# Odd attention of a hybrid encoder: maps combined unnormalised, the RMS norm of each head moved to VectorE, and the first four heads projected ahead of the last four

## What is computed

```python
def one_block(qblk):
    scores = jnp.einsum('bhqd,bhkd->bhqk', qblk, k).astype(F32) * (hd ** -0.5)
    p = jax.nn.softmax(scores, axis=-1).reshape(bsz, h, 2, C_Q_BLOCK, s)
    a = (p[:, :, 0] - lam * p[:, :, 1]).astype(v.dtype)
    return jnp.einsum('bhqk,bhkd->bhqd', a, v)
...
return rms_norm(out, subln_w) * (1.0 - lambda_init)     # per head, over 128 channels
...
return merge_heads(o) @ w_out                            # output projection, 1024 x 1024
```

## Time and profile before

| what | value |
|---|---|
| median of 3 runs | 1373.25 us (1370.11 to 1374.86) |
| the profiled execution, its own time | 1379.12 us |
| its span, first to last instruction | 1377.2 us |
| mean granted TensorE clock | 0.964 |
| odd attention, first combine to last | 502.36 to 533.06 us |
| output projection, first product to last | 546.20 to 570.68 us |

### The profile page before, as it was taken

The page is one execution under the profiler, slowest core; times in us unless marked ns, Lnnn a source line. Parts: engine busy times, 40 slices in busy tenths (PEclk is TensorE's granted clock), DMA queues, the critical chain, the costliest instruction groups (busy, mean ns, idle before and its releaser), DMA issues.

```text
span 1377.2 us, 20147 instructions
## 1 busy us (share of the span) xinstructions
PE 1298.9 (94%) x7164; PEld 1183.8 (86%) x7164; DVE 1069.3 (78%) x1006; ACT 835.8 (61%) x870; POOL 127.1 (9%) x112
## 2 busy tenths in 40 slices
PE   5997899999899986899999999999999999999996
PEld 4887888999787865789899899899998998998984
DVE  4777756544546996778889889889889898898997
ACT  3555342434433463357777777777777777787773
POOL 1035011000001832110000000000000000000000
PEclk9998959999999997889999999999999999999998
DMA  9653027766436540689999999999999999999990
GB/s 337 186 186 94 1 76 259 247 180 192 154 108 191 166 146 1 229 285 385 342 391 377 352 398 358 367 398 346 378 395 337 396 387 346 392 353 359 399 358 32
DMA packets 231280, 374.75 MB, mean 272 GB/s; under 512 B 8784, under 2 KB 156368, under 8 KB 231104
## 3 DMA queue, kind: packets, MB, share of 16 engines
q1 hardware_dynamic: 225344, 351.50, 72.8%
q0 software_dynamic: 5888, 22.61, 4.4%
HBM read 363.07 MB, written 11.01 MB: 272 GB/s over the span
## 4 chain that ended last, share of the span: by engine, by line
PE 85%; DVE 10%; issue 2%; ACT 2%; DMA 1%; POOL 0%; SPq 0%; DVEq 0%; ACTq 0%
PE psum L323 24%; PE psum L325 24%; PE psum L324 24%; DVE wlo L304 4%; PE psum L1710 1%; DMA raw<-in_ev_w_in 1%; PE psum L1528 1%; PE psum L1356 1%; PE psum L1355 1%; PE psum L1354 1%; PE psum L1464 1%; PE psum L1444 1%; PE psum L1512 1%; PE psum L1339 1%; PE psum L1377 1%
## 5 line engine op out<-in xcount | busy, mean ns | idle before, releaser
L304 DVE TENSOR_TENSOR wlo<-raw,whi 128x1408 fp32r<-128x1408 f32 (+2 forms) x493 | 785.4, 1612 | 209.3 <-ACT whi L297 205.6
L297 ACT CAST whi<-raw 128x1408 fp32r<-128x1408 f32 (+2 forms) x493 | 653.2, 1331 | 300.0 <-PE psum L325 275.7
L323 PE MATMUL psum<-whi,xe_hi 128*128 128x352 f32 x1024 | 332.6, 325 | 1.6 <-DVE mv L1299 1.6
L325 PE MATMUL psum<-whi,xe_lo 128*128 128x352 f32 x1024 | 330.7, 323 | 0.0
L324 PE MATMUL psum<-wlo,xe_hi 128*128 128x352 f32 x1024 | 330.5, 323 | 0.0
L323 PEld LDWEIGHTS psum<-whi,xe_hi 128*128 128x128 f32 x1024 | 192.4, 188 | 2.1 <-issue 1.8
L324 PEld LDWEIGHTS psum<-wlo,xe_hi 128*128 128x128 f32 x1024 | 192.4, 188 | 0.3
L325 PEld LDWEIGHTS psum<-whi,xe_lo 128*128 128x128 f32 x1024 | 192.5, 188 | 0.0
L323 PE MATMUL psum<-whi,xT_hi 128*128 128x512 f32 (+1 forms) x464 | 168.2, 363 | 8.4 <-DVE wlo L304 7.0
L324 PE MATMUL psum<-wlo,xT_hi 128*128 128x512 f32 (+1 forms) x464 | 167.5, 361 | 0.0
L325 PE MATMUL psum<-whi,xT_lo 128*128 128x512 f32 (+1 forms) x464 | 167.1, 360 | 0.0
(11 more groups left out here) (281 smaller groups left out, 1289.0 us busy)
## 6 DMA issues: line engine op xcount, KB each, us to landing
raw<-in_od_w SPq DMA_DIRECT2D x256, 704.0 KB, 6.9
raw<-in_od_w SPq DMA_DIRECT2D x94, 768.0 KB, 6.3
raw<-in_ev_w SPq DMA_DIRECT2D x32, 704.0 KB, 4.2
raw<-in_ev_w_in SPq DMA_DIRECT2D x32, 512.0 KB, 5.0
raw<-in_od_w SPq DMA_DIRECT2D x30, 512.0 KB, 6.1
raw<-in_od_w_in SPq DMA_DIRECT2D x24, 512.0 KB, 4.2
raw<-in_ev_w SPq DMA_DIRECT2D x12, 768.0 KB, 4.4
raw<-in_ev_w_out SPq DMA_DIRECT2D x8, 512.0 KB, 4.6
```

The lines of the kernel that those rows point to most:

```text
L297: nc.scalar.copy(into[j][:, 0:kc * n], src[:, 0:kc * n]).then_inc(hi_done, 1)
L304: nc.vector.tensor_tensor(into[j][:, 0:kc * n], src[:, 0:kc * n], high[j][:, 0:kc * n].bitcast(F32), ALU.subtract).then_inc(lo_done, 1)
L323: nc.tensor.matmul(ps, hi[:, k, t0:t0 + P], w_h, start=(k == first_k), stop=False)
L325: last = nc.tensor.matmul(ps, lo[:, k, t0:t0 + P], w_h, start=False, stop=(k == last_k))
```

## The change

The maps are combined unnormalised: with d0 and d1 the sums of a row's two maps, the new map is e1 * (-lambda * d0 / d1) + e0, which is the old one times d0. The factor is taken back in the norm: the sum of squares is multiplied by 1 / d0 squared before the power, and the result of the power by 1 / d0 after it. So `combine` has one small product and one full combination for each row tile and no scaling. The power stays on GpSimd, for both groups of four heads with 8 values per row (`hms`, `hrs`); the multiplication by it and by the gain is now one VectorE instruction for each head and row tile (`normal_heads`), for both groups. The heads are turned and split in two lots (`turn_heads`, `mixed_hi`, `mixed_lo`): the first four after the last values, then tile 0 of the projection (which needs only the first two heads), then the last four heads, then tiles 1 to 3. ScalarE squares the last four heads behind the copies of the first four, and casts tile 0 of the second weight group ahead of the copies of the last four.

```diff
@@ GpSimd @@
-            rms_heads(1, on2, sub[:, None, None, :].broadcast_to([P, NT, 4, 128]), proj2[:, :, 0:512])
-            for t in range(NT):
-                pool.wait_ge(r_ms, 3 + t)
-                rsqrt(vec[:, 40 + 4 * t:44 + 4 * t], vec[:, 32 + 4 * t:36 + 4 * t], 1.0 / AD).then_inc(r_rs, 1)
+            for g in range(2):
+                pool.wait_ge(h_ms, g + 1)
+                rsqrt(hrs[:, g].rearrange("p t h -> p (t h)"), hms[:, g].rearrange("p t h -> p (t h)"), 1.0 / AD).then_inc(h_pw, 1)
@@ ScalarE: map_exps, and behind the head loop @@
-                                         accum_out=vec[:, 48 + 4 * p + u:49 + 4 * p + u]).then_inc(c_e, 1)
+                                         accum_out=den[:, h, u:u + 1]).then_inc(c_e, 1)
...
+            def mixed_hi(g):
+                for t in range(NT):
+                    act.wait_ge(t_ps, 16 + 2 * g + t + 1)
+                    nc.scalar.copy(by_bank(xT_hi, 2 * t + g), psum[:, 4 + 2 * g + t, :].rearrange("p (k s) -> p k s", s=P)).then_inc(t_hi, 1)
+
+            mixed_hi(0)
             act.wait_ge(c_av, 8)
-            act.wait_ge(heads_out, 2)
+            act.wait_ge(h_ms, 1)
             for t in range(NT):
                 nc.scalar.activation(sq2[:, t], psum[:, 6 + t, :].rearrange("p (h c) -> p h c", h=4), ACT.Square).then_inc(r_sq, 1)
-            transposed_hi(4)
-            split_hi(act, Q_OUT2, 1, G_SQ)
+            split_hi(act, Q_OUT2, 1, G_SQ, js=(0,))
+            mixed_hi(1)
+            split_hi(act, Q_OUT2, 1, G_SQ, js=(1, 2, 3))
@@ VectorE: combine @@
-                link(nc.vector.reciprocal(vec[:, 64 + 4 * p:68 + 4 * p], vec[:, 48 + 4 * p:52 + 4 * p]))
-                link(nc.vector.tensor_scalar(vec[:, 80 + 2 * p:82 + 2 * p], vec[:, 66 + 4 * p:68 + 4 * p], vec[:, 92:93], None, ALU.mult))
-                for t in range(NT):
-                    link(nc.vector.tensor_scalar(eP[p][:, 1, t, :], eP[p][:, 1, t, :], vec[:, 80 + 2 * p + t:81 + 2 * p + t], None, ALU.mult))
-                    ins = nc.vector.scalar_tensor_tensor(aP[p][:, t, :], eP[p][:, 0, t, :], vec[:, 64 + 4 * p + t:65 + 4 * p + t],
-                                                         eP[p][:, 1, t, :], ALU.mult, ALU.add)
+                link(nc.vector.reciprocal(rden[:, h, :], den[:, h, :]))
+                link(nc.vector.scalar_tensor_tensor(cmap[:, h, :], rden[:, h, 2:4], vec[:, 92:93], den[:, h, 0:2], ALU.mult, ALU.mult))
+                for t in range(NT):
+                    ins = nc.vector.scalar_tensor_tensor(aP[p][:, t, :], eP[p][:, 1, t, :], cmap[:, h, t:t + 1],
+                                                         eP[p][:, 0, t, :], ALU.mult, ALU.add)
@@ VectorE: the norm @@
+            def mean_squares(g):
+                dve.wait_ge(r_sq, 2 + 2 * g)
+                r0 = rden[:, 4 * g:4 * g + 4, 0:2].rearrange("p h t -> p t h")
+                nc.vector.tensor_tensor(hrs[:, g], r0, r0, ALU.mult)
+                link(nc.vector.tensor_reduce(hms[:, g], sq2, AX_X, ALU.add))
+                nc.vector.tensor_tensor(hms[:, g], hms[:, g], hrs[:, g], ALU.mult).then_inc(h_ms, 1)
+
+            def normal_heads(g):
+                dve.wait_ge(h_pw, g + 1)
+                r0 = rden[:, 4 * g:4 * g + 4, 0:2].rearrange("p h t -> p t h")
+                link(nc.vector.tensor_tensor(hrs[:, g], hrs[:, g], r0, ALU.mult))
+                for t in range(NT):
+                    for h in range(4):
+                        col = g * 512 + h * 128
+                        values = psum[:, 6 + t, h * 128:h * 128 + 128] if g else on2[:, t, h, :]
+                        ins = nc.vector.scalar_tensor_tensor(proj2[:, t, col:col + 128], values, hrs[:, g, t, h:h + 1], sub[:],
+                                                             ALU.mult, ALU.mult)
+                    ins.then_inc(mix_done, 1)
...
                 if h == 5:
-                    sum_squares(1, sq2)
-            dve.wait_ge(heads_out, 2)
-            for t in range(NT):
-                dve.wait_ge(r_sq, 3 + t)
-                nc.vector.tensor_reduce(vec[:, 32 + 4 * t:36 + 4 * t], sq2[:, t], AX_X, ALU.add).then_inc(r_ms, 1)
...
-            transposed_lo(4)
+                    mean_squares(0)
+            normal_heads(0)
+            mixed_lo(0)
+            mean_squares(1)
+            normal_heads(1)
+            mixed_lo(1)
             split_lo(dve, Q_OUT2, 1, G_SQ)
@@ TensorE @@
-            pe.wait_ge(heads_out, 2)
-            transpose_chunks(lambda k, t: proj2[:, t, k * P:(k + 1) * P], mixed=2)
-            square_block(Q_OUT2, 0, 0, turned=20)
+            def turn_heads(g):
+                for t in range(NT):
+                    pe.wait_ge(mix_done, 2 + 2 * g + t + 1)
+                    for kk in range(4):
+                        k = 4 * g + kk
+                        ins = nc.tensor.transpose(psum[:, 4 + 2 * g + t, kk * P:(kk + 1) * P], proj2[:, t, k * P:(k + 1) * P], ident)
+                    ins.then_inc(t_ps, 1)
+
+            turn_heads(0)
+            for j in range(GT):
+                if j in (0, 2):
+                    pe.wait_ge(t_lo, 16 + j + 2)
+                tile_products(pe, Q_OUT2, 0, j, 2, NB, 2 * j, (xT_hi, xT_lo),
+                              [(psum[:, t, :], t * P) for t in range(NT)], 0, KD - 1)
+                if j == 0:
+                    turn_heads(1)
             last_group(Q_OUT2, G_SQ, [2 * j for j in range(GT)], (xT_hi, xT_lo), 2, KD - 1)
```

More of the change, by code:

```diff
@@ L193, in trunk @@
         lamv, d6 = at("lamv", [P, 4, CD], F32, d5)
+        den, d7 = at("den", [P, CH, 4], F32, d6)
+        rden, d8 = at("rden", [P, CH, 4], F32, d7)
+        cmap, d9 = at("cmap", [P, CH, 2], F32, d8)
+        hms, d10 = at("hms", [P, 2, NT, 4], F32, d9)
+        hrs, d11 = at("hrs", [P, 2, NT, 4], F32, d10)
         sq2 = proj2[:, :, D:D + 512].rearrange("p t (h c) -> p t h c", h=4)
@@ L258, in trunk @@
         rope2_pool = sem("rope2_pool")
+        h_ms, h_pw = sem("h_ms"), sem("h_pw")
         lam_x = sem("lam_x")
@@ L1131, in _, with mixed_lo @@
+            def mixed_lo(g):
+                for t in range(NT):
+                    dve.wait_ge(t_hi, 16 + 2 * g + t + 1)
+                    nc.vector.tensor_tensor(by_bank(xT_lo, 2 * t + g), psum[:, 4 + 2 * g + t, :].rearrange("p (k s) -> p k s", s=P),
+                                            by_bank(xT_hi, 2 * t + g).bitcast(F32), ALU.subtract).then_inc(t_lo, 1)
             map_max(0)
```

## The result

The changed kernel takes 1363.65 us (median of 12 runs, 1361.58 to 1369.81), the kernel before 1374.51 (12 runs, 1370.11 to 1378.43). The ratio is 0.9921 with a 95% interval of 0.9905 to 0.9937, so 8.7 to 13.1 us faster. The profiled execution after has a span of 1360.1 us, 17.1 less than before.

What follows compares the result with a forecast made beforehand. VectorE sets the head loop's period at full clock, TensorE at half clock; gains of 5.2 up to the last values and 3.3 in the tail sum to 8.5 us, giving a median of 1364.7 us, range 1360.5 to 1370.0.

Steps and rivals of the forecast that it cites:

- Z: End of the last values' products on TensorE, before the tail; forecast at 532.4 instead of 537.60, 5.2 us earlier.
- the tail: From the last values to the projection's end: tile 0 runs under the last heads' chain, gain 3.3 us.
- Combine, 0.77 per head: VectorE's head loop: two scalings removed per head, 1.28 instead of 2.05 us, period 2.62 instead of 3.39.
- The hold of 3.8 us: Last head's combine: two VectorE instructions slowed beside GpSimd's multiplication of the first four heads; 3.8 us would go.
- The half clock makes the fourth wait for its scores: Early head loop: TensorE at half clock delays the fourth combine to 512.9 instead of 513.05, nothing gained.
- the term of 5.2 us: Gain claimed up to the end of the last values, with half clock as profiled; full clock throughout would give 10.0.
- The first rival: Denser head loop raises TensorE's clock one stretch earlier: 7.4 gained by the last values, 10.7 in all; chance 0.15.
- The last turn and values: TensorE's final transposes and values products, at half clock after the sixth head's values end at 528.0; finished at 532.4.
- a bound with 2.4: Projection after tile 0: if the clock falls again for 12 products after the gap, 2.4 us less gain, 0.9.
- the third rival: Gap after tile 0 costs clock, also for the router's products, and the power holds a combine: gain 2.9, 1370.4; chance 0.12.
- Eight operations of 128 columns at 0.27: First four heads' norm on VectorE: with a small product 2.4 us, hidden while TensorE finishes the last values.
- The power beside a combine: GpSimd's 8-element power, 1.67 us, beside VectorE combines: no price counted; a hold could cost up to 1.7 us.

Runs made afterwards that it cites:

- scaled combine: Changed kernel with the scalings back in each combine and the three small products that undo their absence removed; 1369.28 us, ratio 0.9957 to before.
- squares first, filled: Changed kernel with the last four heads' squares and sum ahead of the first four's split, plus 14 idle TensorE products after the fifth head's values; 1369.43 us.
- the run after: Changed kernel with four unused GpSimd products of 1024 columns from the third combine on, beside whole combines; 1373.42 us, ratio 0.9984 to before.

## Why the prediction was right, and where it was off

**Forecast and measurement.** 1364.7 with 1360.5 to 1370.0 was said, 1363.65 measured; 8.5 us of gain against 10.9; the forecast stands closer to the time than to the gain because the median of before was 1373.25 for 3 runs and is 1374.51 for 12. "Faster" had 0.83. From first combine to the projection's end it is 12.2 where the sum had 8.5, and nearly all of the difference is in one term: up to Z 9.1 us were gained (35.24 to 26.15), not 5.2; the tail gave 3.15 of 3.3.

*Combine, 0.77 per head.* Right in price (1.27 measured, 1.28 said) and in period (2.60 and 2.81 in turn), shown by the scaled combine: 4.6 us of loop.

*The hold of 3.8 us.* Right, shown alone on the kernel before: 4.0 in the loop, 3.8 of it in the last combine.

*"The half clock makes the fourth wait for its scores."* This is the step that failed, and with it the term of 5.2 us. I carried the half clock from the trace of before, unchanged in time. In eight of the ten traces with the new combine the fourth combine starts 8.4 to 8.6 us after the first, in the other two 9.1 and 9.2; I had 10.5, and the four traces with the scalings kept have 10.5 to 10.7. The clock's rise is part of what a denser loop does, not its backdrop: it comes 4.2 to 4.9 us after the first combine in all ten, and 7.6 to 8.0 after it in the four. The half clock lasted 3.4 us in nine of the ten, 6.8 in the tenth (squares first, filled) and in the four. Why the denser loop brings the rise forward is not shown beyond this count. The first rival had the earlier rise, and with it Z 27.8 us after the first combine; 26.15 was measured. My chance of 0.15 for it was too low. The argument against it (the gap around the four heads' square) did not concern this place: that gap, still 2.67 us, comes before the seventh head's turn, and the clock did fall behind it.

*The last turn and values.* Said: Z at 30.0 after the first combine. The clock is at half for 3.4 us there (518.3 to 521.7) and full for the last 1.4 us before Z; I had it at half up to Z.

*The tail, 3.3 us.* 3.15 measured, 29.89 against 29.8 us from Z, but by two errors that cancel. The chain was shorter at full clock: tile 0 at Z + 2.44 instead of 3.35, power done at Z + 6.1 instead of 7.4, tile 1 at Z + 9.1 instead of 10.45. The 84 products then took 20.8 instead of 19.3, since the clock did fall in the gap, which I had as a bound with 2.4. The rule of the Trainium skill that I set beside the third rival (TensorE: Matmul & The Clock Gate, HAM oscillation) held here in kind: after the burst of tile 0 and waits of 2.07 and 0.38 us the clock is at half, and the first seven products of tile 1 are spaced by 0.43 us or more. It cost about 1.4. The length of the wait alone does not decide: in the three kernels with the squares first TensorE waits 3.0 us before tile 0, and the clock is full through tile 0 in the one without a filler and at half in most of it in the two with one. What decides is open.

*Eight operations of 128 columns at 0.27.* 2.19 us for eight, 0.27 each. They lie under the last values as said: the loop to Z doesn't grow.

*The power beside a combine.* Timeline after:

```profile
516.80 1.67 POOL L476 TENSOR_TENSOR hrs<-hrs,neg_half 128x8 f32<-128x8 f32 x1
516.81 0.88 DVE L1138 SCALAR_TENSOR_TENSOR aP<-eP,cmap 128x256 f32<-128x256 f32 x2
...
518.07 0.88 DVE L1138 SCALAR_TENSOR_TENSOR aP<-eP,cmap 128x256 f32<-128x256 f32 x2
```

The two combinations take 0.88 beside it and 0.88 without: the row decided rightly for a power of 8 elements. But what I, and my expectation for the run after, made of it (two-input instructions are free) was wrong in general: beside products of 1024 columns they are held. GpSimd's work differs between these two runs in size (8 columns against 1024) and in operation (a power against a product); which of them decides is open.

*Behind the projection.* 25.2 before, 25.4 to 26.3 in all changed kernels, at half clock for most of it: up to 1.2 us given back. The clock goes with it: where the stretch takes 26.3 us the half clock lasts 20 to 21 us, elsewhere about 17. The experts take 781.3 to 781.4 in every kernel of this study, so nothing else came back.

**Shares of the 12.2 us**, by the single edits: the hold 4.0 (loop alone), the scalings 4.6 in the loop, tile 0 under the last heads 3.0. These make 11.6, but over all stages the same three edits are worth 7.9, 3.4 and 3.0, which is more than 12.2: each moves the clock, too. The kernel before with its norm on VectorE, without any new order of TensorE's work, has a tail of 30.22, so on top of it the new order of the tail gains only 0.3 us, and the new combine 4.7 in the loop, of which 0.7 is given back up to Z. The shares therefore depend on the order in which they are taken.

## What to carry to other kernels

Carry a clock state through a forecast as something that the change can move: where TensorE gets denser work at 1.2 GHz, work the loop through once with the rise where it was and once with it earlier, and give both a real chance. When large products stand on GpSimd beside a VectorE-bound loop, look for VectorE rows far over their usual duration, and count the hold and the wait that it makes for TensorE. When a long chain (square, sum, power, product, transposes) ends last, start its first step before everything that only feeds work which has slack.

## What the runs showed of the hardware that I had not expected

A VectorE instruction of two columns with two SBUF inputs took 1.85 us beside a GpSimd product of 1024 columns, and two of 256 columns 4.23 together (0.22 and 0.88 alone); a reduction out of PSUM kept its 1.22, and beside a power of 8 columns two of 256 columns kept their 0.88. Three idle products in the wait before the seventh head's turn kept the clock full there, and it fell 6.7 us later instead (counted from the first combine), for as long, with no gain in all. Float32 products of 384 columns were carried out as two instructions each, 0.32 us apart from start to start.
